# First loads in smaller pieces with x ahead on the scalar engine's queue; the last two slots of the last token tile in halves

## The chip, the cores and the metric

One Trainium2 chip, one core. The time is that of the device for one execution of the whole program, in microseconds (us), the median of three runs. The core has TensorE (PE in the profile, its weight loads PEld), VectorE (DVE), ScalarE (ACT), GpSimd (POOL) and SyncE (SP, which here only issues transfers).

## What is computed

The reference runs two blocks on x, 256 tokens by 2048 columns in float32. The first has a state-space layer (S5) and a sparse-attention layer, the second an attention layer with two kinds of heads and an MLP. Only the two ends matter here:

```python
def s5_mixer(x, w_in, lam_re, lam_im, log_dt, b_re, b_im, c_re, c_im, d_skip, w_glu, b_glu, w_out):
    u, z = jnp.split(x @ w_in, 2, axis=-1)       # the kernel's first work: u, in four groups of columns
    dt = jnp.exp(log_dt.astype(f32))[:, None]     # tables of the state space, from small parameters
    mag = jnp.exp(lr * dt)
    ar = mag * jnp.cos(li * dt)
    ai = mag * jnp.sin(li * dt)
...
def second_block(x, ...):
...
        h = rmsnorm(x, ln2[l])
        x = x + jnp.square(jax.nn.relu(h @ w_mlp_in[l])) @ w_mlp_out[l]
    return rmsnorm(x, ln_f)                        # the kernel's last work
```

## The kernel before

**Weights.** All large matrix products go through one stream of weights. A unit is a block of 2048 by 512 weights in eight slots; a slot holds two row tiles of 128 by 512. SP brings slot after slot into `RAW` (`slot`, line 414). ACT rounds a slot into `WH` (`high`, the group L1195), DVE forms the remainder `WL` (`low`, L1824), and PE multiplies in three passes (high by high, high by low, low by high). One slot's work on PE is called a tick, and `lo_ready` tells PE that the slot's two parts are there. Ticks are numbered through the program; `beside(tau)` on PE and on ACT puts other small work behind tick tau. Each engine runs its own list in the order in which it is written; nothing else sets the order.

**The start.** `WHOLE = 6`: ticks 0 to 5 don't wait for the split. They multiply the raw float32 weights in `whole_tick` (L657), eight instructions a tick. They need x with columns in partitions. PE turns 128 by 128 pieces of x (`transposes`, L639: four for each index i, which is one pair of row tiles, and so one tick), ACT copies each turned pair to `XF` (`x_cols`, L1234, two copies for each i), and the semaphore `tr_tmp` lets the tick of that number start. Before the first transposes PE runs `WARM = 5` matmuls on zeros (L664). x comes in four pieces of 512 columns (`x_piece`, 512 KB), each for two ticks. SP issues the first behind a small piece of the constants, then the weight slots, with x pieces 1 to 3 between them. ACT's queue issues the small parameters (log_dt, lam_re, lam_im).

Beside this run the tables of the state space. PE turns the parameters (`params_turn`, L674), the first of them between the two halves of tick 0; ACT copies them (L1226) and takes an exponential (L1356); then DVE starts a long list of its own (`angles`, L1887, then `turns`, `base_products`, `base_turns`, `factors`, `coefficients`, `powers`, `b_powers`), in which also stand the remainders of x (`rounding_left`, L1865: each waits for ACT's rounding of x, L1241) and those of the weights of ticks 6 to 9 (L1824). ACT's rounding of the first two pairs (`rounded(0, 2)`) stands in its list behind `x_cols(2, 4)`, so behind the copies of x piece 1.

**The end.** In the last unit the work is done for token tile 0 and then for tile 1 in slots 4 to 7 (`tiles_apart`, L581; matmuls of 512 columns, weights moving). For each tile DVE adds the last product to x (L2853), sums squares (L2854), POOL takes the root (`rsqrt`, L2895), and then DVE scales columns 1024 to 1535 (L2857) and scales and multiplies by the gain columns 1536 to 2047 (L2859), while ACT scales columns 0 to 1023 (L1804). The columns 0 to 1535 have been multiplied by the gain before. SP stores the two pieces of DVE (256 KB each), ACT's queue the half of ACT (512 KB). The program ends when SP has seen all six stores land.

## Time and profile before

| | us |
|---|---|
| median of three runs (2005.87 to 2006.30) | 2006.16 |
| span of the profiled execution, first to last instruction | 2003.7 |
| PE busy | 1991.7 |
| DVE busy | 1317.6 |
| ACT busy | 981.9 |
| POOL busy | 73.8 |
| TensorE clock granted, mean | 0.999 |

The span is counted from the first instruction to the last; the median of the runs lies 2.5 us above it, for what stands around the instructions. In a timeline row the first two numbers are the start and the length of a group in us from the span's start, `x8` is how many records it holds (a float32 matmul leaves two records, a transpose one), and brackets tell how long the engine was idle before it and what ended that. A "q" behind an engine's name (SPq, ACTq) marks work of its sequencer, such as issuing a transfer.

### The profile page before, as it was taken

How to read it: one execution, taken by the hardware profiler on the slowest of the kernel's cores; microseconds unless marked ns; L12 is line 12 of the kernel's file. 1: busy time of each engine (PE TensorE's matmuls, PEld its weight loads, DVE VectorE, ACT ScalarE, POOL GpSimd, SP SyncE). 2: the span in 40 equal slices, each digit the busy share in tenths (PEclk: the TensorE clock that was granted, in tenths of full speed). 3: DMA queues.
4: the chain of work that ended last, by engine and by line, in shares of the span. 5: the costliest groups of instructions: out<-in, count | busy, mean ns of one | idle time of the engine just before them, and what ended most of it. 6: DMA issues, size and time to landing. Idle time of an engine off the chain costs nothing.

```text
span 2003.7 us, 30858 instructions
## 1 busy us (share of the span) xinstructions
PE 1991.7 (99%) x11849; PEld 1735.5 (87%) x11849; DVE 1317.6 (66%) x1931; ACT 981.9 (49%) x1444; POOL 73.8 (4%) x84
## 2 busy tenths in 40 slices
PE   9999999999999999999999999999999999999998
PEld 8998789988888888888999988888888888888887
DVE  7998877566666666578767766555555555555555
ACT  5664555354545454455456446544344434434443
POOL 2000132000000000100000001000000000000000
PEclk9999999999999999999999999999999999999999
DMA  9346578546464545756555555566666666666663
GB/s 293 96 152 234 164 214 250 165 131 189 126 195 131 182 145 169 247 154 199 169 168 148 155 171 191 178 189 190 194 188 190 193 191 189 189 195 181 196 192 107
DMA packets 203220, 360.74 MB, mean 180 GB/s; under 512 B 25393, under 2 KB 33937, under 8 KB 202449
## 3 DMA queue, kind: packets, MB, share of 16 engines
q1 hardware_dynamic: 200944, 351.82, 57.5%
q0 software_dynamic: 1664, 5.97, 0.9%
q8 instruction: 94, 1.54, 0.3%
q10 hardware_dynamic: 480, 1.10, 0.1%
q14 instruction: 38, 0.30, 0.0%
...
## 4 chain that ended last, share of the span: by engine, by line
PE 90%; DVE 7%; issue 1%; ACT 1%; DMA 0%; POOL 0%; POOLq 0%; DVEq 0%; ACTq 0%; SPq 0%
PE acc L529 36%; PE acc L533 10%; PE banks L563 9%; PE acc L563 9%; PE banks L529 8%; PE banks L566 4%; PE acc L566 4%; DVE w_high_low L1824 2%; PE banks L983 1%; PE acc L657 1%; PE banks L956 1%; PE acc L581 1%; PE acc L603 1%; PE banks L969 1%; PE banks L1035 1%
## 5 line engine op out<-in xcount | busy, mean ns | idle before, releaser
L1824 DVE TENSOR_TENSOR w_high_low<-raw,w_high_low 128x1024 fp32r<-128x1024 f32 x650 | 794.6, 1231 | 599.6 <-ACT w_high_low L1195 597.2
L1195 ACT ACTIVATE w_high_low<-raw 128x1024 fp32r<-128x1024 f32 x650 | 684.0, 1059 | 707.7 <-PE acc L529 292.9
L529 PE MATMUL acc<-w_high_low,x_high_low 128*128 128x512 f32 x1608 | 387.1, 396 | 0.4 <-DVE w_high_low L1824 0.4
L529 PEld LDWEIGHTS acc<-w_high_low,x_high_low 128*128 128x128 f32 x1608 | 299.5, 188 | 63.0 <-issue 0.8
L529 PE MATMUL acc<-w_high_low,h_high 128*128 128x512 f32 x1088 | 292.1, 390 | 0.1
L533 PE MATMUL acc<-x_high_low,w_high_low 128*128 128x256 f32 x2160 | 273.5, 285 | 0.0
L533 PEld LDWEIGHTS acc<-x_high_low,w_high_low 128*128 128x128 f32 x2160 | 263.4, 191 | 1.6
L563 PE MATMUL acc<-x_high_low,w_high_low 128*128 128x512 f32 x768 | 241.9, 396 | 0.4
L563 PE MATMUL banks<-x_high_low,w_high_low 128*128 128x512 f32 x768 | 241.2, 395 | 0.0
L529 PEld LDWEIGHTS acc<-w_high_low,h_high 128*128 128x128 f32 x1088 | 203.0, 188 | 41.8 <-issue 0.5
L566 PEld LDWEIGHTS banks<-x_high_low,w_high_low 128*128 128x128 f32 x768 | 144.3, 188 | 34.1
L566 PEld LDWEIGHTS acc<-x_high_low,w_high_low 128*128 128x128 f32 x768 | 144.3, 188 | 34.0
L529 PE MATMUL acc<-w_high_low,h_low 128*128 128x512 f32 x544 | 167.6, 389 | 0.0
L566 PE MATMUL acc<-x_high_low,w_high_low 128*128 128x256 f32 x768 | 150.9, 278 | 0.0
L566 PE MATMUL banks<-x_high_low,w_high_low 128*128 128x256 f32 x768 | 150.9, 278 | 0.0
L529 PE MATMUL banks<-w_high_low,h_high 128*128 128x512 f32 x480 | 128.3, 389 | 0.0
L529 PEld LDWEIGHTS acc<-w_high_low,h_low 128*128 128x128 f32 x544 | 102.1, 188 | 21.3
L563 PEld LDWEIGHTS acc<-x_high_low,w_high_low 128*128 128x128 f32 x768 | 117.6, 189 | 1.9 <-DVE x_rows L2205 1.0
L563 PEld LDWEIGHTS banks<-x_high_low,w_high_low 128*128 128x128 f32 x768 | 116.9, 189 | 0.0
L529 PEld LDWEIGHTS banks<-w_high_low,h_high 128*128 128x128 f32 x480 | 90.1, 188 | 18.7
L529 PE MATMUL banks<-w_high_low,h_low 128*128 128x512 f32 x240 | 73.9, 389 | 0.0
L529 PEld LDWEIGHTS banks<-w_high_low,h_low 128*128 128x128 f32 x240 | 45.0, 188 | 9.4
...
## 6 DMA issues: line engine op xcount, KB each, us to landing
raw<-in_b_w_in SPq DMA_DIRECT2D x128, 512.0 KB, 3.8
raw<-in_w_mlp_in SPq DMA_DIRECT2D x128, 512.0 KB, 3.7
raw<-in_w_mlp_out SPq DMA_DIRECT2D x128, 512.0 KB, 4.5
raw<-in_w_in SPq DMA_DIRECT2D x96, 512.0 KB, 4.0
raw<-in_kv_w SPq DMA_DIRECT2D x48, 512.0 KB, 4.2
raw<-in_a_w_in SPq DMA_DIRECT2D x32, 512.0 KB, 6.6
raw<-in_b_w_out SPq DMA_DIRECT2D x32, 512.0 KB, 4.7
raw<-in_w_out SPq DMA_DIRECT2D x32, 512.0 KB, 4.7
```

The lines of the kernel that those rows point to most:

```text
L529: ins_ = nc.tensor.matmul(PAIRS[pair][:, t, :], xa[:, kt + j, t * P:(t + 1) * P], wa[:, k, j, :], start=first and n == 0, stop=last and n ...
L533: ins_ = nc.tensor.matmul(ACC[pair][:, m // 2, (m % 2) * TOK:(m % 2 + 1) * TOK], wa[:, k, j, m * P:(m + 1) * P], xa[:, kt + j, :], start=f ...
L563: nc.tensor.matmul(both, WH[:, k, j, m * P:(m + 1) * P], XX[:, 2 * s + j, :, :].rearrange("p c t -> p (c t)"), start=s == 0 and j == 0, st ...
L566: ins_ = nc.tensor.matmul(both[:, 0:TOK], WL[:, k, j, m * P:(m + 1) * P], XH[:, 2 * s + j, :], start=False, stop=s == SLOTS - 1 and j == 1 ...
L581: ins_ = nc.tensor.matmul(PAIRS[pair][:, t, :], xa[:, kt, t * P:(t + 1) * P], wa[:, s % SPLIT, j, :], start=start and s == SPLIT and j == ...
L603: ins_ = nc.tensor.matmul(PAIRS[group % 2][:, t, :], xa[:, 2 * s + j, t * P:(t + 1) * P], wa[:, k, j, :], start=s == 0 and j == 0 and n == ...
L657: ins_ = nc.tensor.matmul(ACC[0][:, m // 2, (m % 2) * TOK:(m % 2 + 1) * TOK], RAW[:, s, j, m * P:(m + 1) * P], XF[kt // 8][:, kt % 8, :], ...
L956: ins_ = nc.tensor.matmul(BK[n % 2][:, lo:lo + w], QT[:, h, t * P:(t + 1) * P], keys[:, g:g + 1, 0:w].rearrange("p o k -> p (o k)"), start ...
L969: ins_ = nc.tensor.transpose(BK[2][:, b * P:(b + 1) * P], PB_[:, n % 2, b * P:(b + 1) * P], ID)
L983: ins_ = nc.tensor.matmul(BK[3][:, t * P:(t + 1) * P], PTB[:, n % 2, b * P:(b + 1) * P], v[:, k, g * HD:(g + 1) * HD], start=b < 2, stop=b ...
L1195: nc.scalar.activation(WH[:, s % SPLIT, :, :], RAW[:, s, :, :], ACT.Copy).then_inc(hi_ready, WHOLE + 1 if first_one else 1)
L1824: V.tensor_tensor(WL[:, k, :, :], RAW[:, p % SLOTS, :, :], WH[:, k, :, :].bitcast(F32), ALU.subtract).then_inc(lo_ready, WHOLE + 1 if isin ...
```

## The change

At the start, x piece 0 is cut in two. Its first 256 columns are issued by ACT's queue, ahead of the parameters; SP issues slot 0 as two transfers with the rest of x piece 0 between them. PE waits for the first half of x (`x_ahead`), turns only pair 0, and runs tick 0, each half of it when its half of the weights is there. Pair 1 is turned behind tick 0 together with the first parameters; x piece 1 and the second parameters, which were turned behind tick 0, are turned behind tick 1. ACT's list has the copies of pair 1 at the head of what it does beside tick 0. One warming matmul is left out.

At the end, slots 6 and 7 of tile 1 are done for columns 0 to 255 of the last group first, and then for columns 256 to 511 into a bank of their own. DVE adds the whole product so far and squares the first half while PE does the second; then it adds and squares the second half. The gain is multiplied while POOL takes the root. The last scaling is split at column 896: ACT does 0 to 895, DVE 896 to 2047 in one instruction, and each is stored by one transfer.

```diff
--- before.py
+++ after.py
@@ -52,7 +52,8 @@
 LAST_ROOT, LAST_TILE = 6, 3
-WARM = 5
+LAST_COLS = 896
+WARM = 4
@@ -436,8 +438,11 @@
-        x_piece(0)
-        for s in range(SLOTS):
+        first_w = rows_cols(A_IN, 0, 0)
+        sp.dma_start(RAW[:, 0, 0, :], first_w[:, 0, :]).then_inc(w_first, 16)
+        sp.dma_start(X[:, :, 2 * P:COLS], x_in[:, :, 2 * P:COLS]).then_inc(x_first[0], 16)
+        sp.dma_start(RAW[:, 0, 1, :], first_w[:, 1, :]).then_inc(raw_in[0], 16)
+        for s in range(1, SLOTS):
             slot(U_AIN, s, rows_cols(A_IN, 2 * P * s, 0))
@@ -505,19 +510,17 @@
-        for t in range(NT):
-            for c in (2, 3):
-                sp.wait_ge(out_ready, 2 * t + c - 1)
-                cols = slice(c * COLS, (c + 1) * COLS)
-                sp.dma_start(out[0, t * P:(t + 1) * P, cols], X[:, t, cols]).then_inc(stored, 16)
-        sp.wait_ge(stored, 16 * 3 * NT)
+        for n, (t, c0, c1) in enumerate(((0, 2 * COLS, 3 * COLS), (0, 3 * COLS, DM), (1, LAST_COLS, DM))):
+            sp.wait_ge(out_ready, n + 1)
+            sp.dma_start(out[0, t * P:(t + 1) * P, c0:c1], X[:, t, c0:c1]).then_inc(stored, 16)
+        sp.wait_ge(stored, 16 * 5)
@@ -569,10 +572,28 @@
+        def last_halves(pair, kt0, free):
+
+            for half in range(2):
+                cols = slice(half * COLS // 2, (half + 1) * COLS // 2)
+                bank = ACC[0][:, 0, 0:COLS // 2] if half else PAIRS[pair][:, 1, cols]
+                if half:
+                    pe.wait_ge(acc_free, free)
+                for s in (SLOTS - 2, SLOTS - 1):
+                    for j in range(2):
+                        kt = kt0 + 2 * (s - SPLIT) + j
+                        for n, (xa, wa) in enumerate(((HH, WH), (HH, WL), (HL, WH))):
+                            ins_ = nc.tensor.matmul(bank, xa[:, kt, P:2 * P], wa[:, s % SPLIT, j, cols],
+                                                    start=half == 1 and s == SLOTS - 2 and j == 0 and n == 0,
+                                                    stop=s == SLOTS - 1 and j == 1 and n == 2, skip_group_check=True)
+                ins_.then_inc(slot_used if half else tile_full, 2 if half else 1)
+
-        def tiles_apart(unit, pair, kt0, start, xh, xl):
+        def tiles_apart(unit, pair, kt0, start, xh, xl, halves=False):
 
             for t in range(NT):
                 for s in range(SPLIT, SLOTS):
+                    if halves and t and s >= SLOTS - 2:
+                        continue
@@ -647,12 +668,13 @@
-            pe.wait_ge(raw_in[s], 16)
+            if s:
+                pe.wait_ge(raw_in[s], 16)
             pe.wait_ge(tr_tmp, TR_X + s + 1)
             for j in range(2):
                 kt = 2 * s + j
-                if kt == 1:
-                    params_turn(0)
+                if s == 0:
+                    pe.wait_ge(*((raw_in[0], 16) if j else (w_first, 16)))
@@ -663,7 +685,8 @@
         pe.wait_ge(const_in, 16)
-        x_turn(0)
+        pe.wait_ge(x_ahead, 16)
+        transposes(TR_X, X, None, 0, 1)
@@ -777,6 +800,10 @@
             if tau == 0:
+                pe.wait_ge(x_first[0], 16)
+                transposes(TR_X, X, None, 1, 2)
+                params_turn(0)
+            if tau == 1:
                 x_turn(1)
                 params_turn(1)
@@ -1214,6 +1243,8 @@
+        x_in = ins["x"][0].rearrange("(t p) d -> p t d", p=P)
+        act.dma_start(X[:, :, 0:2 * P], x_in[:, :, 0:2 * P]).then_inc(x_ahead, 16)
         act.dma_start(LDT[64:96, :], ins["a_log_dt"][0].rearrange("(s w) -> s w", w=2)).then_inc(dt_in, 16)
@@ -1240,7 +1271,7 @@
-        x_cols(0, 2)
+        x_cols(0, 1)
@@ -1351,6 +1382,7 @@
             if tau == 0:
+                x_cols(1, 2)
                 params_copy(1, 1)
@@ -1801,9 +1833,10 @@
-            nc.scalar.activation(X[:, t, 0:DM // 2], X[:, t, 0:DM // 2], ACT.Copy, scale=RSTD[:, t:t + 1]).then_inc(last_scaled, 1)
+            cols = slice(0, LAST_COLS if t else DM // 2)
+            nc.scalar.activation(X[:, t, cols], X[:, t, cols], ACT.Copy, scale=RSTD[:, t:t + 1]).then_inc(last_scaled, 1)
@@ -2844,27 +2877,47 @@
+        def last_tile():
+            xr = X[:, 1, 3 * COLS:]
+            v.wait_ge(tile_full, LAST_TILE + 1)
+            steps.link(V.scalar_tensor_tensor(xr, PAIRS[3][:, 1, :], RSTD[:, 5:6], xr, ALU.mult, ALU.add))
+            for half in range(2):
+                xr = X[:, 1, 3 * COLS + half * COLS // 2:3 * COLS + (half + 1) * COLS // 2]
+                if half:
+                    v.wait_ge(slot_used, SLOTS * (U_MLP + 32))
+                    steps.link(V.scalar_tensor_tensor(xr, ACC[0][:, 0, 0:COLS // 2], RSTD[:, 5:6], xr, ALU.mult, ALU.add))
+                before_, sum_ = (MS[:, NT:NT + 1], MS[:, 1:2]) if half else (MS[:, NT + 1:NT + 2], MS[:, NT:NT + 1])
...
+            v.wait_ge(ms_rows, LAST_ROOT + 1)
+            xr = X[:, 1, 3 * COLS:]
+            steps.link(V.tensor_tensor(xr, xr, GF[:, 3 * COLS:], ALU.mult))
+            v.wait_ge(rstd_rows, LAST_ROOT + 1)
+            xr = X[:, 1, LAST_COLS:]
+            V.tensor_scalar(xr, xr, RSTD[:, 1:2], None, ALU.mult, ALU.bypass).then_inc(out_ready, 1)
```

In DVE's part tile 0 keeps the old steps under the name `first_tile`, and in the call of the last unit `last_halves` follows `tiles_apart(..., halves=True)`.

PE's list at the start, before (L639 transposes of x, L657 the raw ticks, L674 parameters):

```order
3 L639 MATMUL banks<-constants,x_rows 128x128 [waits x_first0,const_in]
4 L639 MATMUL banks<-constants,x_rows 128x128 x7
5 L657 MATMUL acc<-x_cols_90,raw 128x256 [waits tr_tmp,raw_in0]
6 L657 MATMUL acc<-x_cols_90,raw 128x256 x3
7 L674 MATMUL acc<-constants,param_rows 128x128 [waits ssm_in,rows_set]
8 L657 MATMUL acc<-x_cols_90,raw 128x256 x4
9 L639 MATMUL banks<-constants,x_rows 128x128 [waits x_first1]
10 L639 MATMUL banks<-constants,x_rows 128x128 x7
11 L674 MATMUL acc<-constants,param_rows 128x128 [waits params_in]
12 L657 MATMUL acc<-x_cols_90,raw 128x256 [waits tr_tmp,raw_in1]
13 L657 MATMUL acc<-x_cols_90,raw 128x256 x7
14 L657 MATMUL acc<-x_cols_90,raw 128x256 [waits tr_tmp,raw_in2]
```

and after (L660 transposes, L679 the raw ticks, L697 parameters):

```order
3 L660 MATMUL banks<-constants,x_rows 128x128 [waits x_ahead,const_in]
4 L660 MATMUL banks<-constants,x_rows 128x128 x3
5 L679 MATMUL acc<-x_cols_90,raw 128x256 [waits w_first,tr_tmp]
6 L679 MATMUL acc<-x_cols_90,raw 128x256 x3
7 L679 MATMUL acc<-x_cols_90,raw 128x256 [waits raw_in0]
8 L679 MATMUL acc<-x_cols_90,raw 128x256 x3
9 L660 MATMUL banks<-constants,x_rows 128x128 [waits x_first0]
10 L660 MATMUL banks<-constants,x_rows 128x128 x3
11 L697 MATMUL acc<-constants,param_rows 128x128 [waits ssm_in,rows_set]
12 L679 MATMUL acc<-x_cols_90,raw 128x256 [waits tr_tmp,raw_in1]
13 L679 MATMUL acc<-x_cols_90,raw 128x256 x7
14 L660 MATMUL banks<-constants,x_rows 128x128 [waits x_first1]
```

The eight transposes of x piece 0 have become four, four more stand directly ahead of tick 1, those of x piece 1 directly ahead of tick 2, and the first parameters stand behind all of tick 0.

ACT's list at the start, after, from the copies of pair 1 on (L1265 copies of turned x, L1257 copies of turned parameters, L1388 the exponential that DVE waits for, L1272 rounding of x; before, the same rows stood in the same order, as L1234, L1226, L1356 and L1241):

```order
9 L1265 ACTIVATE x_cols_90<-banks 128x256 [waits tr_full]
10 L1265 ACTIVATE x_cols_90<-banks 128x256
11 L1257 ACTIVATE param_cols<-acc 128x128 [waits params_full]
12 L1388 ACTIVATE ssm_params<-param_cols 128x32 [waits params_done]
13 L1265 ACTIVATE x_cols_90<-banks 128x256 [waits tr_full]
14 L1265 ACTIVATE x_cols_90<-banks 128x256
15 L1265 ACTIVATE x_cols_90<-banks 128x256 [waits tr_full]
16 L1265 ACTIVATE x_cols_90<-banks 128x256
17 L1257 ACTIVATE param_cols<-acc 128x128 [waits params_full]
18 L1272 ACTIVATE x_high_low<-x_cols_90 128x2x256 [waits tr_tmp] x2
```

Nothing moved within this list, but the transposes that its copies of pair 1, and of pairs 2 and 3, wait for are now done by PE one tick later.

The last instructions of DVE, after (L2894 to L2912 are token tile 1, in the lines of the new `last_tile`):

```order
1309 L2894 SCALAR_TENSOR_TENSOR x_rows<-banks,rstd,x_rows 128x512
1310 L2901 ISA normed_rows,mean_squares<-x_rows,mean_squares 128x256
1311 L2901 ISA mean_squares 128x1
1312 L2899 SCALAR_TENSOR_TENSOR x_rows<-acc,rstd,x_rows 128x256
1313 L2901 ISA normed_rows,mean_squares<-x_rows,mean_squares 128x256
1314 L2901 ISA mean_squares 128x1
1315 L2909 TENSOR_TENSOR x_rows<-x_rows,last_gain 128x512
1316 L2912 TENSOR_SCALAR x_rows<-x_rows,rstd 128x1152
```

where before there stood for tile 1:

```order
1309 L2853 SCALAR_TENSOR_TENSOR x_rows<-banks,rstd,x_rows 128x512
1310 L2854 ISA normed_rows,mean_squares<-x_rows,mean_squares 128x512
1311 L2854 ISA mean_squares 128x1
1312 L2857 TENSOR_SCALAR x_rows<-x_rows,rstd 128x512
1313 L2859 SCALAR_TENSOR_TENSOR x_rows<-x_rows,rstd,last_gain 128x512
```

The sum and the squares are in halves of 256 columns, and the two scalings of 512 columns have become a gain and one scaling of 1152.

## Rows read from the trace of the kernel before

**Rows 1.** Page, its first lines: span and busy time of the engines.
```profile
span 2003.7 us, 30858 instructions
...
PE 1991.7 (99%) x11849; PEld 1735.5 (87%) x11849; DVE 1317.6 (66%) x1931; ACT 981.9 (49%) x1444; POOL 73.8 (4%) x84
```

**Rows 2.** Waits of PE in the whole span: total, times, longest, in us.
```profile
PE banks L639 <- DMA x_rows<-in_x: 0.6, 1, 0.6
...
PE acc L657 <- ACT x_cols L1234: 0.4, 1, 0.4
```

**Rows 3.** Transfers issued in 0 to 1.3 us: KB, us to landing.
```profile
x_rows<-in_x SPq DMA_DIRECT2D x1, 512.0 KB, 4.3
constants<-in_consts SPq DMA_DIRECT2D x1, 72.0 KB, 2.2
...
param_rows<-in_a_lam_re ACTq DMA_DIRECT2D x1, 16.0 KB, 4.2
```

**Rows 4.** Timeline of the start, PE and ACT around ticks 0 and 1.
```profile
0.75 0.42 ACTq L1217 DMA_DIRECT2D log_dt_rows<-in_a_log_dt  x1
...
1.20 3.87 PE L664 MATMUL banks<-products_a 128*128 128x256 f32 x10 [1.20 <-DVE products_a L1874]
...
1.21 0.42 SPq L437 DMA_DIRECT2D x_rows<-in_x  x1
...
5.70 1.06 PE L639 MATMUL banks<-constants,x_rows 128*128 128x128 f32 x8 [0.63 <-DMA x_rows<-in_x]
...
6.36 1.21 ACT L1234 ACTIVATE x_cols<-banks 128x256 f32<-128x256 f32 x4 [2.38 <-PE banks L639]
...
7.16 1.97 PE L657 MATMUL acc<-x_cols,raw 128*128 128x256 f32 x8 [0.40 <-ACT x_cols L1234]
...
10.80 1.04 PE L639 MATMUL banks<-constants,x_rows 128*128 128x128 f32 x8
...
11.44 1.21 ACT L1234 ACTIVATE x_cols<-banks 128x256 f32<-128x256 f32 x4 [1.63 <-PE banks L639]
...
11.79 7.07 PE L657 MATMUL acc<-x_cols,raw 128*128 128x256 f32 x32
...
12.67 1.18 ACT L1241 ACTIVATE x_high_low<-x_cols 128x512 fp32r<-128x512 f32 x2
```

**Rows 5.** The same timeline, DVE's list and PE up to tick 9.
```profile
9.84 0.19 DVE L1887 TENSOR_TENSOR ssm_params<-param_cols,ssm_params 128x32 f32<-128x32 f32 x1 [6.82 <-ACT ssm_params L1356]
...
14.01 1.29 DVE L1865 TENSOR_TENSOR x_high_low<-x_cols,x_high_low 128x512 fp32r<-128x512 f32 x2
...
38.66 6.02 PE L533 MATMUL acc<-x_high_low,w_high_low 128*128 128x256 f32 x48
...
40.09 2.39 DVE L1824 TENSOR_TENSOR w_high_low<-raw,w_high_low 128x1024 fp32r<-128x1024 f32 x2
```

**Rows 6.** Waits of DVE between 9.8 and 42 us: total, times, longest.
```profile
DVE x_high_low L1865 <- ACT x_high_low L1241: 0.3, 1, 0.3
```

**Rows 7.** Timeline of the end, token tile 1.
```profile
1995.77 0.62 PE L581 MATMUL banks<-w_high_low,h_high 128*128 128x512 f32 x2
1996.23 0.39 PE L581 MATMUL banks<-w_high_low,h_low 128*128 128x512 f32 x1
...
1996.65 0.75 DVE L2853 SCALAR_TENSOR_TENSOR x_rows<-banks,rstd,x_rows 128x512 f32<-128x512 f32 x1 [1.33 <-PE banks L581]
...
1997.44 0.75 DVE L2854 CUSTOM_DVE_ANT_0 normed_rows<-x_rows,mean_squares 128x512 f32<-128x512 f32 x1
...
1998.87 0.49 DVE L2857 TENSOR_SCALAR x_rows<-x_rows,rstd 128x512 f32<-128x512 f32 x1 [0.67 <-POOL rstd L2895]
...
2000.11 0.37 ACTq L1806 DMA_DIRECT2D out<-x_rows  x1
```

**Rows 8.** Groups of DVE by line and shape: count, busy, mean ns, idle before.
```profile
L1843 DVE CUSTOM_DVE_ANT_0 banks<-banks,constants 128x256 f32<-128x256 f32 x48 | 22.3, 465 | 0.0
...
L2760 DVE SCALAR_TENSOR_TENSOR x_high_low<-banks,param_cols,x_high_low 128x256 fp32r<-128x256 f32 x16 | 6.5, 474 | 0.4 <-ACT x_high_low L1748 0.4
```

46 lines of the change are left out of this document (26 added, 20 removed).

## The prediction

> **What bounds the kernel now.** The page's first lines come first: PE is busy 1991.7 of 2003.7 us [rows 1], so whatever moves PE's first or last instruction moves the end one for one, and nothing in between has slack to give back. The list of PE's waits says the same: only tenths of a microsecond anywhere, the largest at the start, for x and then for ACT's copy of the turned x [rows 2]. The change touches only the two ends, so the stretch before PE's first real multiply and the stretch behind its last are to be costed, and one question more: does every engine that PE needs shortly after the start keep up? For that the timeline of the first 45 us is read for DVE [rows 5]. DVE starts its list at 9.84 us, when ACT has the first parameters, and from there to 41.3 us it waits once, for 0.3 us [rows 6]. So in this stretch DVE bounds itself, and the remainder of the weights of tick 9 stands in that list: L1824 runs from 40.09, two in 2.39 us, the first done at 41.3. PE runs ticks 8 and 9 from 38.66, 48 matmuls in 6.02 us, so it asks for tick 9 at 38.66 + 2.95 = 41.6. The margin is 0.3 us. That is the row on which this prediction turns: a PE that is early there gains 0.3 us at most, and a late DVE is paid in full.
>
> **Start, step 1: x arrives earlier.** The first transfer of x (512 KB) is issued at 1.21 and lands 4.3 us later; PE starts turning at 5.70 and multiplies at 7.16 [rows 3, 4]. Now 256 KB go out at 0.75, where the first parameter stood on ACT's queue. Early bound: 72 KB took 2.2 us and 512 KB took 4.3 [rows 3]; by bytes 256 KB take 3.1 and land at 3.9, but PE then still warms up: ten records from 1.20 to 5.07, two of them fewer now, some 4.6. Late bound: half of slot 0 travels beside it, so the same 512 KB are under way and the time stays 4.3, landing at 5.05, PE at 5.2. I take PE at 4.85, nearer the early end, since the second queue starts at once and its half doesn't wait for all of the other. The first multiply then comes at 4.85 + 1.46 = 6.3 in place of 7.16: -0.85 (between -1.05 and -0.5). The warming matmul left out costs nothing: PE waited 0.63 us behind it.
>
> The Trainium skill (Trainium Kernel Development and Optimization, Key Constraints) says that transfers issued from several engines share the same 16 DMA engines, and that this saves only the time of issue. By that rule the late bound would hold, and the result would be 0.35 us higher than the one below. No row of before shows two large loads side by side on two queues.
>
> **Step 2: PE waits for ACT twice.** Turning a pair, copying it on ACT and starting the tick takes 1.46 us where nothing hides it: 5.70 to 7.16, with ACT starting 0.66 after PE [rows 4]. Before, this was paid once; pair 1 was turned in its shadow, and pairs 2 and 3 were turned a whole tick ahead. Between tick 0 and tick 1 there stand 0.99 us (10.80 to 11.79), and ticks 1 and 2 run on as one row. Now pair 1 is turned directly ahead of tick 1 and pair 2 directly ahead of tick 2. Ahead of tick 1: 1.45 in place of 0.99, less 0.1 for the parameters that no longer stand inside tick 0: +0.35. Ahead of tick 2: 1.45 where nothing stood, with the refilled pipeline +1.5. Together +1.85. The transposes of x pieces 2 and 3 stay where they were. With step 1 PE asks for everything behind tick 2 1.0 us later than before, so at tick 9 at 42.6.
>
> **Step 3: DVE starts later.** Its list began 9.84 - 7.16 = 2.7 us behind the first multiply. Now the parameters are turned behind all of tick 0 and copied behind ACT's copies of pair 1: tick 0 3.54, then 0.64 until ACT starts, 0.6 for two copies, 0.3 for the parameters' copy, 0.26 for the exponential: 5.3 behind 6.3, so 11.6. That is +1.8.
>
> **Step 4: and then it waits for ACT.** At 14.01 DVE takes the remainder of x (L1865), which needs ACT's rounding L1241. That started at 12.67, 1.87 us behind the first transpose of x piece 1, and half of its 1.18 is needed [rows 4, 5]. It stands behind the copies of that piece, which PE now turns behind tick 1: 6.3 + 3.54 + 1.45 + 3.5 = 14.8. The rounding starts at 16.7, its first half is done at 17.35, DVE goes on at 17.4. Alone DVE would have been there at 15.8. So the list is late by 17.4 - 14.0 = 3.4 us from here. Its one later wait, 0.3 us, goes, since ACT is then less late than DVE [rows 6]. The remainder for tick 9 is done at 41.3 + 3.4 - 0.3 = 44.4.
>
> **Sum of the start.** PE asks at 42.6 and gets it at 44.4; before it went on at 41.6. Start: +2.8 us. Queued behind tick 9 on PE is all the rest of the program, and PE has no idle time in it that could give this back.
>
> **The end.** PE: 12 matmuls of 512 columns at 0.23 (1995.77 to 1996.23 are two) become 24 of 256 at 0.123 (6.02 for 48): +0.2 [rows 5, 7]. DVE behind the last matmul: sum and squares of 512 columns take 0.75 each; of 256 columns the same kinds took 0.47 [rows 7, 8]: -0.55. The root is there 0.4 us earlier. The first half's work (0.75 + 0.47) lies beside PE's last 12 matmuls (1.5 us), and so costs nothing; were that cover gone, it would cost up to 1.2. Then the stores. The gain (512 columns, no more than the 0.75 of the scaling with gain) lies beside POOL's root but ends some 0.1 behind it. DVE's scaling of 512 columns took 0.49; for 1152 it is between 0.85 (a fixed part of 0.2) and 1.1 (by columns). Before, DVE's first store could go when its first scaling ended, 1999.36; now its only store goes between 1999.45 and 1999.65, while ACT's goes 0.5 earlier than 2000.11 (0.4 of the root, 0.1 of 128 fewer columns). The same 1 MB is stored. If bytes bound it, the end is +0.1 to +0.3; if the last queue to start bounds it, -0.5. I take 0.0 between the two, since one transfer moves each way.
>
> **The rivals.** (1) *x comes late on ACT's queue, and the kernel is slower.* The 16 KB of lam_re, second on that queue, took 4.2 us, as long as 512 KB on SP's [rows 3]. If ACT's queue gets so small a share beside the weights, x lands later, and every microsecond is paid: all of steps 2 to 4 hang on the first multiply. From a landing at 5.9 us on the result is slower by over 0.2%; with 6.6 it is 2.8 + 1.9 = +4.7, 2010.9. For it speaks that row; against it that lam_re was behind another transfer and x now is first. (2) *DVE doesn't hold PE at tick 9*, because the rounding isn't late or PE is later than I think. It decides when DVE's lateness is under 1.3 us. What is left is PE's own +1.0: 2007.2. Against it speaks the margin of 0.3 us and a DVE without waits. (3) *The gain shows*: ACT's copies are hidden after all, step 2 costs nothing and DVE keeps its margin: -0.85 at the start and -0.5 at the end, 2004.8. Against it speaks that the 1.46 us stand in the trace for just this sequence.
>
> **How the numbers follow.** The profiled span of 2003.7 becomes 2006.5. The runs lie 2.5 us above the span for what surrounds it, which the change doesn't touch: 2006.16 + 2.8 + 0.0 = 2009.0. Its own range takes in the bounds of step 1 (-0.2 to +0.35), the end (-0.5 to +0.3) and some 0.3 for steps 2 to 4: 2008.0 to 2010.0. About 0.2%, 4.0 us, is what a measurement of this kernel can tell from no change; so this forecast is within it, though on the slow side. Chances: forecast 0.62, rival 1 0.13, rival 2 0.12, rival 3 0.08, something else 0.05. Slower by over 0.2%, above 2010.2: rival 1, the rest and a tail of the forecast's, 0.16. Faster by over 0.2%, under 2002.1: no case reaches it, 0.02. The range leaves out rival 3 and the far part of rival 1: 2007.0 to 2010.5.
>
> **What would show it.** Step 1: the first transpose between 4.6 and 5.2 us. Step 2: PE waits of some 0.9 us ahead of tick 1 and 0.5 ahead of tick 2, on ACT's copies. Steps 3 and 4: DVE's list starts at about 11.6, and L1865's successor waits 1.5 us for the rounding. The sum: PE waits at tick 9 for DVE, for 1 us or more together with shorter waits at ticks 6 and 7, and goes on near 44.4. The end: a root 1.8 us behind the last matmul in place of 2.2, and both stores issued within 0.3 us. If DVE goes on at L1865 without a wait, step 4 is wrong and the sum falls by about 1.5; if the granted clock is low in the first ticks, all of it is too low.

## The result, and the profile after

The changed kernel takes 2012.76 us (2010.95 to 2012.93, six runs) where the kernel before takes 2006.23: 1.0031 times as long, with a 95% interval of 1.0021 to 1.0041. The forecast was 2009.0, with a range up to 2010.5: so it had the direction right, but its +2.8 us is less than half of the 6.5 us measured. The six runs fall into two groups, two near 2011 and four near 2012.8. The profiled execution is one of the first group, 2010.95 us with a span of 2009.1, and all readings below are of it unless another is named. Nine later runs of the same code (below) gave 2010.9 to 2011.8 eight times and 2012.9 once. So the median of 2012.76 is one of the upper group, and what follows explains first the 5.4 us of the lower one.

The page's first lines and PE's list of waits, as in [rows 1, 2] (total, times, longest, in us):

```profile
span 2009.1 us, 30884 instructions
...
PE 1992.7 (99%) x11859; PEld 1735.7 (86%) x11859; DVE 1325.1 (66%) x1934; ACT 981.6 (49%) x1444; POOL 73.8 (4%) x84
```

```profile
PE acc L536 <- DVE w_high_low L1857: 2.5, 2, 1.8
PE acc L679 <- DMA raw<-in_a_w_in: 1.4, 2, 0.9
...
PE acc L679 <- ACT x_cols L1265: 1.0, 2, 0.7
```

Two waits are new, for DVE's remainders of the weights (L1857 is before's L1824) and for the first weights, and the wait for ACT's copies of x has grown from 0.4 to 1.0 us. The timeline of PE at the start answers [rows 4, 5] (start, us busy, and in brackets the idle time before; the last row of the first block is cut by the window's end, tick 1 goes on behind it):

```profile
4.43 0.60 PE L660 MATMUL banks<-constants,x_rows 128*128 128x128 f32 x4
5.97 1.97 PE L679 MATMUL acc<-x_cols,raw 128*128 128x256 f32 x8 [0.95 <-DMA raw<-in_a_w_in]
8.39 1.99 PE L679 MATMUL acc<-x_cols,raw 128*128 128x256 f32 x8 [0.45 <-DMA raw<-in_a_w_in]
10.22 0.60 PE L660 MATMUL banks<-constants,x_rows 128*128 128x128 f32 x4
10.66 0.27 PE L697 MATMUL acc<-constants,param_rows 128*128 128x128 f32 x1
11.66 2.61 PE L679 MATMUL acc<-x_cols,raw 128*128 128x256 f32 x11 [0.73 <-ACT x_cols L1265]
```

```profile
34.27 6.27 PE L536 MATMUL acc<-x_high_low,w_high_low 128*128 128x256 f32 x48 [1.84 <-DVE w_high_low L1857]
...
46.30 3.13 PE L536 MATMUL acc<-x_high_low,w_high_low 128*128 128x256 f32 x24 [0.68 <-DVE w_high_low L1857]
```

PE turns x 1.3 us earlier than before and multiplies 1.2 us earlier, and yet it goes on at tick 9 at 46.3 in place of 41.6, 4.7 us late. By tick 4 PE itself is 1.5 us late (25.36, before 23.90); the rest comes in its two waits for DVE, ahead of ticks 6 and 9, and since DVE hands over tick 9's weights only at 46.2, it is DVE's lateness that counts. DVE's own timeline of the same stretch, the four rows that matter, and POOL's one row:

```profile
11.98 0.19 DVE L1920 TENSOR_TENSOR ssm_params<-param_cols,ssm_params 128x32 f32<-128x32 f32 x1 [3.34 <-ACT ssm_params L1388]
...
17.75 1.29 DVE L1898 TENSOR_TENSOR x_high_low<-x_cols,x_high_low 128x512 fp32r<-128x512 f32 x2 [1.50 <-ACT x_high_low L1272]
...
25.42 0.43 DVE L1912 TENSOR_SCALAR rotation_base<-rotation_base 128x512 f32<-128x512 f32 x1
25.89 1.99 DVE L1943 TENSOR_SCALAR rotation_base<-rotation_base 128x512 f32<-128x512 f32 x1
```

```profile
25.58 4.04 POOL L2944 MEMSET c_powers<- 128x2048 f32 x2 [17.02 <-PE banks L660]
```

The list starts 2.1 us late, waits 1.5 us for ACT's rounding (late by 3.7), and then one operation of 0.43 us takes 1.99 (late by 5.3), while POOL zeroes c_powers. In the kernel before, the same operation and the same zeroing stood apart:

```profile
22.14 0.43 DVE L1910 TENSOR_SCALAR rotation_base<-rotation_base 128x512 f32<-128x512 f32 x1
```

```profile
24.12 3.55 POOL L2891 MEMSET c_powers<- 128x2048 f32 x2 [15.56 <-PE banks L639]
```

The end, which answers [rows 7]:

```profile
2001.40 0.28 PE L586 MATMUL acc<-w_high_low,h_low 128*128 128x256 f32 x1
...
2002.83 0.69 DVE L2909 TENSOR_TENSOR x_rows<-x_rows,last_gain 128x512 f32<-128x512 f32 x1
2002.88 1.06 POOL L2948 TENSOR_TENSOR rstd<-mean_squares,minus_half 128x1 f32<-128x1 f32 x1 [3.83 <-DVE mean_squares L2901]
2004.03 1.04 ACT L1837 ACTIVATE x_rows<-x_rows,rstd 128x896 f32<-128x896 f32 x1 [3.74 <-POOL rstd L2948]
2004.05 0.82 DVE L2912 TENSOR_SCALAR x_rows<-x_rows,rstd 128x1152 f32<-128x1152 f32 x1 [0.52 <-POOL rstd L2948]
...
2005.11 0.37 ACTq L1839 DMA_DIRECT2D out<-x_rows  x1
```

POOL's root starts earlier behind the last matmul (1.2 us behind its end, before 1.7) but takes 1.06 in place of 0.56, so that it ends 2.26 behind it (before 2.2). So the budget of the profiled execution is: tick 9 +4.7, from there to the last matmul +0.4 (some 0.2 of it are the halves), from the last matmul to the end of the span +0.3 (7.4 in place of 7.1). Together +5.4, the difference of the spans.

### The profile page after: what moved, and what is told of

The parts are those of the page before. It is cut to its first block, busy times and chain, and to the rows that moved or that the text cites. A ratio compares the mean times of both kernels' runs of the same rounds, so it can differ in the third digit from the quotient of the medians.

```text
span 2009.1 us, 30884 instructions
## 1 busy us (share of the span) xinstructions
PE 1992.7 (99%) x11859; PEld 1735.7 (86%) x11859; DVE 1325.1 (66%) x1934; ACT 981.6 (49%) x1444; POOL 73.8 (4%) x84
## 3 DMA queue, kind: packets, MB, share of 16 engines
q0 software_dynamic: 1664, 5.97, 0.9%
## 4 chain that ended last, share of the span: by engine, by line
PE 88%; DVE 9%; issue 2%; ACT 1%; DMA 0%; SPq 0%; POOL 0%; POOLq 0%; DVEq 0%; ACTq 0%
PE acc L532 35%; PE acc L536 9%; PE banks L566 9%; PE acc L566 9%; PE banks L532 8%; PE banks L569 4%; PE acc L569 4%; DVE w_high_low L1857 2%; PE banks L1010 1%; PE banks L983 1%; PE acc L602 1%; PE acc L624 1%; PE banks L996 1%; PE banks L1062 1%; PE banks L1086 0%
## 5 line engine op out<-in xcount | busy, mean ns | idle before, releaser
L1857 DVE TENSOR_TENSOR w_high_low<-raw,w_high_low 128x1024 fp32r<-128x1024 f32 x650 | 797.0, 1235 | 598.3 <-ACT w_high_low L1224 595.9
```

Of the source, the lines that this page charges most:

```text
L1857: V.tensor_tensor(WL[:, k, :, :], RAW[:, p % SLOTS, :, :], WH[:, k, :, :].bitcast(F32), ALU.subtract).then_inc(lo_ready, WHOLE + 1 if isin ...
```

## The experiments

All times below are medians, and each is set beside runs of the kernel before on the same chip at the same time (2005.7 to 2006.0). Not all experiments ran on the same chip, so two of them are compared by their distance from the kernel before. The intervals of the ratios are about 0.001 to either side, 2 us; differences of a few tenths are read from medians and from traces, and are called so.

### The start alone, and what in it costs

**e1_start.** The diff without its end part.

> The start part of the change alone (split loads, x ahead on ACT's queue, one warming matmul fewer, pair 1 and the parameters turned behind tick 0); the end is as in the kernel before. Theory A: in the profiled run of the changed kernel PE reaches tick 9 4.7 us late (46.30 in place of 41.64), and that is all the start costs. So this kernel takes 2006.2 + 4.7 = 2010.9 us in the same kind of run, and its PE starts tick 9 at about 46.3. The changed kernel's runs fall in two groups, near 2011 and near 2012.8; if the second group is one more DVE operation that waits for a zeroing of POOL (1.9 us each), this kernel shows it as well, and its other group lies at 2012.8 less 0.5. Rival B: the lateness of the first ticks is given back later in the program, and the end part makes most of the loss: then this kernel is within 1.5 us of 2006.2.

Measured: 2011.08 us (2009.83 to 2012.3, 7 runs) against 2005.86, ratio 1.0028 (1.0017 to 1.0040); PE at tick 9 at 45.79 in the profiled run of 2009.83. The start costs 5.2 us in the median and nothing of it is given back: the span minus the start of tick 9 is 1962.2 here, and before 2003.7 - 41.6 = 1962.1. Theory A holds. Two of the seven runs, 2012.2 and 2012.3, form an upper group here as well, and e2_end (below) has none above 2007.1, so that group comes from the start, not from the end.

**e3_memset_later.** As e1_start, and POOL's zeroing waits for DVE:

```
         pool.wait_ge(tr_full, TR_X + 8)
+        pool.wait_ge(tab_dve, 3)
         for i in range(2):
             GP.memset(CX[i][:, :, :, :, :, :], 0.0).then_inc(zeroed, 1)
```

> As e1_start, but POOL's two zeroings of c_powers wait until DVE is through with its rotation_base operations. Theory A (DVE's TENSOR_SCALAR of 128x512 stands still for as long as POOL zeroes: 1.99 us at 25.89 in the changed kernel, 0.43 in the kernel before): that operation takes 0.43 again, the remainder for tick 9 is done 1.56 us earlier, at 44.7, PE starts tick 9 at 44.7, and the time is 2006.2 + 3.1 = 2009.3 us in all runs, with no second group. Rival B (the 1.99 us come from something else, such as a late operand): the time stays that of e1_start, 2010.9 or 2012.5.

Measured: 2009.13 us (2008.47 to 2010.52, 10 runs), 2.0 under e1_start in the median and 1.4 from fastest run to fastest. Its DVE and POOL rows:

```profile
27.14 0.43 DVE L1893 TENSOR_SCALAR rotation_base<-rotation_base 128x512 f32<-128x512 f32 x1
27.61 0.43 DVE L1924 TENSOR_SCALAR rotation_base<-rotation_base 128x512 f32<-128x512 f32 x1
27.95 1.29 DVE L1879 TENSOR_TENSOR x_high_low<-x_cols,x_high_low 128x512 fp32r<-128x512 f32 x2
```

```profile
28.16 3.55 POOL L2906 MEMSET c_powers<- 128x2048 f32 x2 [19.57 <-DVE rotation_base L1924]
```

The operation is back at 0.43, and so is POOL's zeroing at 3.55 (4.04 beside it). TENSOR_TENSOR at 27.95 runs beside the zeroing and is not longer than elsewhere. Theory A holds in its main point. That there would be no second group was wrong: two of ten runs, the profiled one among them, lie at 2010.5, and this profile tells why (below, under the clock).

**e8_memset_collides.** The other direction: the kernel before, with POOL's early zeroings moved beside DVE's rotation_base operations.

```
+        pool.wait_ge(tr_full, TR_X + 6)
         GP.memset(BB[:, :, :, :, :, :], 0.0).then_inc(zeroed, 1)
```

> The kernel before, but POOL zeroes b_powers, tap_blocks and decay only behind the turning of the sixth pair of x, at about 19.7 us instead of 6.0, beside DVE's rotation_base operations. Theory A (a TENSOR_SCALAR of DVE stands still while POOL zeroes): one of the TENSOR_SCALAR between 19.3 and 20.2 takes some 1.3 to 1.8 us in place of 0.43, while TENSOR_TENSOR beside the same zeroing keeps its 0.69; the list is late by about 1.3 us, tick 9 by about 1.0, time 2006.9 to 2007.4 us. Rival B (no such standing still): 2005.9, and all TENSOR_SCALAR at 0.43.

Measured: 2006.82 us (2005.84 to 2008.01, 10 runs) against 2005.99, ratio 1.0004 (0.9995 to 1.0013). The profiled run is a low one, 2005.9. There the zeroing started at 20.01, inside the second of two operations (19.82 to 20.25), which kept its length; the two that started beside a zeroing got longer:

```profile
19.36 0.89 DVE L1879 TENSOR_SCALAR rotation_base<-rotation_base 128x512 f32<-128x512 f32 x2
...
21.74 0.53 DVE L1879 TENSOR_SCALAR rotation_base<-rotation_base 128x512 f32<-128x512 f32 x1
22.30 0.92 DVE L1910 TENSOR_SCALAR rotation_base<-rotation_base 128x512 f32<-128x512 f32 x1
```

```profile
20.01 1.98 POOL L2887 MEMSET b_powers<- 128x2048 f32 x1 [13.94 <-PE banks L639]
21.94 1.01 POOL L2888 MEMSET tap_blocks<- 128x768 f32 x1
22.89 0.39 POOL L2889 MEMSET decay<- 128x8 f32 x1
```

Both of the later ones are longer than 0.43, and each of POOL's zeroings is longer too: 8 elements took 0.39 here, 0.14 in the kernel before. In the changed kernel it is the same: the operation at 25.42 was running when the zeroing began at 25.58 and kept its 0.43, the next one took 1.99. TENSOR_TENSOR at 20.28 and 21.01 stood beside the same zeroing at 0.69 each. In eight of ten runs the time is about 0.6 us or more over the kernel before's median; that in them the zeroing started ahead of the earlier operation is likely, but they have no trace. Theory A's mechanism holds in the trace. Its sizes don't: no operation took 1.3 us, and the 0.8 us of the medians are less than its 0.9 to 1.4 and within the interval.

The Trainium skill (SBUF — State Buffer, Who interferes with whom) states this rule: VectorE and GpSimd share a pair of SBUF ports as an exclusive lock, and `tensor_scalar` and `copy` can run in a mode that takes it, while a VectorE instruction with two SBUF inputs contends only with a GpSimd instruction that reads SBUF. These rows agree with both halves of it: TENSOR_SCALAR at 1.99 beside a zeroing, TENSOR_TENSOR at 0.69. It is a rule by which such a meeting has a price, and the forecast didn't weigh it.

**e5_rounding_first.** As e1_start, and ACT rounds pairs 0 and 1 ahead of its copies of pairs 2 and 3:

```
+                rounded(0, 2)
                 x_cols(2, 4)
                 params_copy(2, 0)
-                rounded(0, 2)
```

> As e1_start, but ACT rounds pairs 0 and 1 of x before it copies pairs 2 and 3, so DVE's first remainders of x find their operand. Theory A: DVE's wait of 1.50 us at 16.2 goes; the list is then only 2.1 us late and its last rotation_base operation ends before POOL's zeroing starts at 25.6, so that the stall of 1.56 goes too. DVE is then 4.93 - 1.50 - 1.56 = 1.9 us late at tick 9, PE itself asks 1.5 us late: tick 9 at 43.2, time 2006.2 + 1.6 = 2007.8 us. Rival B (the wait is only replaced by another, since the copies of pairs 2 and 3 now come later and PE's tick 2 with them): no gain against e1_start, 2010.9 or more. Rival C (only the wait goes, the stall stays): 2009.4.

Measured: 2007.34 us (2007.15 to 2008.91, 10 runs), 3.7 under e1_start in the median and 2.7 from fastest run to fastest, ratio to the kernel before 1.0008 (0.9998 to 1.0017). DVE waits for no rounding of x, and its operation takes 0.43 at 26.02. POOL's zeroing, which starts when PE has turned the last pair, then comes behind it (27.32). The profiled run is the highest of the ten, 2008.91; in it everything from tick 1 on stands some 2 us later (below, under the clock). Theory A holds: the wait of 1.5 us was worth twice its length or more, since it moved the list by just so much that it met the zeroing.

**e4_order.** As e1_start with all its loads; pair 1 and the parameters are turned between the halves of tick 0, pairs 2 and 3 directly behind it:

```
                 if s == 0:
+                    if j:
+                        pe.wait_ge(x_first[0], 16)
+                        transposes(TR_X, X, None, 1, 2)
+                        params_turn(0)
                     pe.wait_ge(*((raw_in[0], 16) if j else (w_first, 16)))
...
             if tau == 0:
-                pe.wait_ge(x_first[0], 16)
-                transposes(TR_X, X, None, 1, 2)
-                params_turn(0)
-            if tau == 1:
                 x_turn(1)
                 params_turn(1)
```

> As e1_start with its loads, but PE turns pair 1 and the first parameters between the two halves of tick 0, and pairs 2 and 3 directly behind tick 0 as in the kernel before. Theory A (the loss is one of order on PE, not of the loads): the first multiply stays at 5.97, the first parameters are turned at about 8.1 and DVE's list starts at about 9.4 in place of 11.98 (before: 9.84), without the waits for rounding and without the stall; tick 9 at 41.3, time 2005.9 us (between 2005.5 and 2006.3). Rival B (the loads in small pieces land later, slot 1 at 9.56 in place of 8.29, and PE pays for that): tick 1 starts later than 11.79 and the time is 2007 us or more.

Measured: 2006.14 us (2005.45 to 2007.59, 10 runs), 4.9 under e1_start, ratio 1.0003 (0.9993 to 1.0013). Seven runs lie at 2005.5 to 2006.4, three at 2007.5. In the profiled run, a low one, the list starts at 9.64, tick 1 at 11.71 and tick 9 at 41.56. So theory A: the loads in smaller pieces and on ACT's queue cost nothing that can be measured, apart from what lifts the three high runs; the loss comes from where PE does the turning. The parameters were turned at 8.70, not at 8.1, and not because they had landed late:

```profile
5.09 3.56 DVE L1890 COPY param_rows<-log_dt_rows 32x128 f32<-32x128 f32 x1 [3.95 <-DMA log_dt_rows<-in_a_log_dt]
```

This copy of 32x128 took 0.22 us in the kernel before. Now log_dt lands at 5.1 us instead of 2.8, and the copy runs until 8.64, when POOL's zeroings of b_powers, tap_blocks and decay (6.01 to 8.57) are over. The changed kernel's copy does the same (5.10 to 8.64), and there POOL's rows are:

```profile
4.91 0.57 POOL L2937 DMA_DIRECT2D head_gains<-in_diff_head_norm  x1
5.48 0.54 POOL L2937 DMA_DIRECT2D head_gains<-in_sb_head_norm  x1
6.01 1.82 POOL L2939 MEMSET b_powers<- 128x2048 f32 x1
```

So it is the same standing still, with one thing open: the copy starts 0.9 us ahead of the first zeroing, while POOL issues its last two transfers, and doesn't end there. In the kernel before it took 0.22 at 2.80, also while POOL was issuing transfers. Why it didn't end before 6.01 is not shown. In the changed kernel it costs nothing, because the parameters are turned only at 10.66.

### The second group: the clock in tick 0

In the profiled runs of e3_memset_later (2010.52 us, where eight others lay at 2008.5 to 2009.4) and of e5_rounding_first (2008.91, others 2007.2 to 2007.9), tick 0 took longer. The timeline of PE in e3_memset_later:

```profile
1.20 3.78 PE L670 MATMUL banks<-products_a 128*128 128x256 f32 x8 [1.20 <-DVE products_a L1888]
4.77 1.06 PE L644 MATMUL banks<-constants,x_rows 128*128 128x128 f32 x4
6.58 5.52 PE L663 MATMUL acc<-x_cols,raw 128*128 128x256 f32 x16 [0.75 <-ACT x_cols L1247]
```

16 matmuls in 5.52 us, where e1_start and the kernel before need 3.7 and 3.8; seven of the first eight have 634 ns records, as the warming matmuls at 1.2 GHz do, the last ones 379 as at 2.4 GHz. The trace's record of the granted clock starts, at its full level, only at 10.26 us here (10.29 in e5_rounding_first), but at 4.1 to 6.3 us in every profile of the changed kernel that there is, and at 4.15 in the kernel before. PE had gone idle for 0.75 us at 5.83 without the clock having risen. That alone doesn't make a late rise: in h4_changed_look (below) PE went idle for the same 0.75 us at 5.84, and the record starts at 6.34. The changed kernel has one warming matmul fewer, and the forecast said that this costs nothing.

**g1_warm5.** The changed kernel with `WARM = 5`.

> The changed kernel with one thing undone: five warming matmuls, as before, in place of four. Theory W: the granted clock rises to its full level only after PE has been kept busy for a while; in the kernel before it rose at 4.15 us, in the profiled run of the changed one at 4.07, but in two of four profiled variants with four warming matmuls PE had gone idle first and the clock rose only at 10.3 us, with tick 0 taking 5.4 us in place of 3.6. That is the second group of the changed kernel's runs. With five warming matmuls at least 8 of 10 runs lie near 2011 us and the median falls from 2012.8 to about 2011.0; spans near 2009.1. Rival X (the groups come from when x and the weights land, or from how DVE and POOL meet): the groups and the median of about 2012 stay.

Measured: 2011.58 us (2011.03 to 2011.98, 8 runs): no run near 2012.8, as theory W had it, but none under 2011.0 either, and the median is 0.6 above the 2011.0 expected. In the profiled run the warming lasts until 5.83 and the first multiply stands at 7.31.

**g2_warm4.** The kernel before with `WARM = 4`.

> The kernel before with one warming matmul fewer, nothing else. Theory W: a part of its runs, some 3 to 7 of 10, finds the clock low when tick 0 starts; tick 0 then takes 5.4 us in place of 3.6, and since the margin at tick 9 is 0.3 us these runs take some 1.5 us more, 2007.4; the others stay at 2005.9. Rival Y (my forecast: the matmul left out costs nothing, since PE waited 0.63 us behind it): all runs at 2005.9, like the kernel before.

Measured: 2005.92 us (2005.42 to 2007.48, 10 runs) against 2005.99. The median stays, as my forecast had it, but three runs lie at 2006.96 to 2007.48, and none of the 31 runs of the kernel before beside them is above 2006.86 (of the 28 beside the first four experiments one was, at 2007.32). One matmul less costs nothing in seven runs of ten and about 1 to 1.5 us in three. The profiled run is a low one although its clock record starts only at 7.13: turning x takes 1.90 us there in place of 1.06, and the first multiply stands at 7.32 in place of 7.16.

**i2_before_warm3.** The kernel before with `WARM = 3`.

> The kernel before with three warming matmuls in place of five. Theory W: more of the runs than with four (3 of 10 above 2006.9) find the low clock; the low tick 0 costs up to 1.9 us less the margin of 0.3 at tick 9: median 2006.5 to 2007.5. My forecast's view (a warming matmul costs nothing as long as PE waits behind it): 2005.8, like the kernel before.

Measured: 2007.36 us (2005.99 to 2008.1, 10 runs) against 2005.72, ratio 1.0007 (0.9997 to 1.0017). In its profiled run PE is idle 1.9 us ahead of x:

```profile
6.03 1.94 PE L639 MATMUL banks<-constants,x_rows 128*128 128x128 f32 x8 [1.91 <-DMA x_rows<-in_x]
7.96 2.74 PE L657 MATMUL acc<-x_cols,raw 128*128 128x256 f32 x8
```

Turning takes 1.94 us in place of 1.06 and half of tick 0 takes 2.74 in place of 1.97. The clock's record starts at 9.54, and tick 9 at 43.2 in place of 41.6. Theory W holds here: in the kernel before, leaving out two warming matmuls costs 1.6 us in the median although PE waits behind them, and nine of the ten runs lie above all 17 runs of the kernel before beside them. Three of the ten spend 0.3 to 1.1 us more than the usual 1.8 outside the span, the profiled one the most; by spans the loss is 1.3 us.

**h2_filled.** The changed kernel, its four warming matmuls kept and two more where PE was idle:

```
         transposes(TR_X, X, None, 0, 1)
+        for n in range(2):
+            nc.tensor.matmul(BK[3][:, 0:TOK], T1[:, 0, 0:P], T1[:, 0, 0:TOK], start=True, stop=True)
```

> The changed kernel, four warming matmuls as it has, and two more between the turning of pair 0 and the first multiply, where PE was idle for 0.95 us. Theory W: the low clock of tick 0 needs this idle time; without it no run lies near 2012.8, all are between 2010.7 and 2011.8, median 2011.2. Rival X: 2 or more of the runs lie above 2012.3, as in the changed kernel (5 of 13 so far).

Measured: 2011.15 us (2010.65 to 2011.49, 8 runs), no run above 2011.5, as theory W had it.

**i1_warm3.** The changed kernel with `WARM = 3`.

> The changed kernel with three warming matmuls in place of four. Theory W: PE is idle sooner and longer before its first multiply, so most runs find the low clock there: the median is 2012.8 or a little more, and the profiled run shows matmuls of 634 ns in tick 0, the clock rising near 10 us, DVE's list starting at about 13.7 in place of 11.98, the operation of 1.99 us as before, tick 9 near 48.2. Rival X (the second group is not the clock's): the median stays at 2011.3 with the same share of high runs.

Measured: 2011.53 us (2010.31 to 2012.2, 8 runs), clock's record from 5.45, tick 0 at 379 ns. Here theory W missed: one warming matmul less did not make the low clock the rule.

**a1_changed_again, h3_changed_look, h4_changed_look.** The changed kernel itself once more, 7, 1 and 1 runs.

> The changed kernel once more, for a second look at its two groups of runs. Theory W: each run near 2012.8 is one in which the granted clock had not risen by the time PE went idle ahead of its first multiply. If the profiled run falls there, its records show matmuls of 634 ns in tick 0 in place of 379, a rise of the clock near 10.3 us, DVE's list starting at about 13.7 in place of 11.98, still with the 1.99 us operation, and PE at tick 9 near 48.2 in place of 46.3. Rival X: a run near 2012.8 has a tick 0 of 3.6 us and loses its 1.9 us elsewhere, for instance in a second DVE operation that stands still.

> The changed kernel, one more profile, in case it falls into the group near 2012.8. Theory W: if the time is near 2012.8 the clock rises near 10.3 us, tick 0 takes 5.4 us and DVE's list starts at about 13.7; if it is near 2011 the clock rises before 7 us.

> As h3_changed_look, one more profile with the same expectation: near 2012.8 with a late rise of the clock, or near 2011 with an early one.

Measured: 2011.33 (2010.9 to 2012.91), 2011.18 and 2011.31 us. No profiled run fell into the upper group. Their clock records start at 4.74, 5.00 and 6.34 us; PE turns x at 4.76 to 4.78 in them and multiplies at 6.11 to 6.58.

So: that a late rise of the clock costs 1 to 2 us and makes high runs is shown by one profiled run each of e3, e5 and i2. That it is what lifted four of the first six runs of the changed kernel is only argued: the amount fits (5.5 in place of 3.7 us for tick 0), and g1 and h2 are without high runs, but with one high run among the nine later ones of the changed kernel the absence in eight proves little, and i1 speaks against it. Which chip the first six ran on is not on record, and the nine later ones ran on two, so that the share of high runs could depend on that too. This stays open.

The last profiles show one more cost. Of h3_changed_look, by stretches (us, PE busy, granted clock, DMA share, GB/s):

```profile
34.00:36.00 2.00, 1.65 (x13) 0.93 1.06 424
36.00:38.00 2.00, 2.00 (x11) 0.50 0.83 321
38.00:40.00 2.00, 2.00 (x15) 0.72 0.12 28
```

Behind PE's 1.84 us of waiting for DVE at tick 6 the granted clock falls to half, 1.2 GHz, and tick 7 runs at that. a1, h2 and i1 show the same; the first profile, e1, g1 and h4 don't. From the start of tick 6 to that of tick 9 it takes 12.4 us (34.35 to 46.74) in place of 12.0 (34.27 to 46.30): a wait may cost more than its length, here 0.4 us more.

### The end

**e2_end.** The end part alone, the start as before.

> The end part of the change alone (last two slots of the last token tile in halves, squares by halves, gain beside the root, 896 columns on ACT and 1152 on DVE); the start is as before. From the profile of the changed kernel: PE's last matmul 0.25 later, the root done 2.26 us behind it in place of 2.22 although it starts earlier (POOL's power took 1.06 in place of 0.56 beside DVE's gain), last store issued at the same distance, its landing 0.4 later. Theory E: +0.5 us, 2006.4 against 2005.9. My forecast was 0.0 (between -0.5 and +0.3).

Measured: 2006.64 us (2006.27 to 2007.06, 11 runs) against 2005.99, +0.65, ratio 1.0003 (0.9994 to 1.0012), so theory E's +0.5 and not the 0.0 of the forecast, as far as medians tell; the root takes 1.06 again and ends 2.26 behind the last matmul's end.

**e6_halves_only.** e2_end without the new scaling: sum and squares in halves, then DVE's two operations, ACT's 1024 columns and the three stores as before (of the diff, DVE's part).

```
...
-            v.wait_ge(ms_rows, LAST_ROOT + 1)
-            xr = X[:, 1, 3 * COLS:]
-            steps.link(V.tensor_tensor(xr, xr, GF[:, 3 * COLS:], ALU.mult))
             v.wait_ge(rstd_rows, LAST_ROOT + 1)
-            xr = X[:, 1, LAST_COLS:]
-            V.tensor_scalar(xr, xr, RSTD[:, 1:2], None, ALU.mult, ALU.bypass).then_inc(out_ready, 1)
+            xr = X[:, 1, 3 * COLS:]
+            V.tensor_scalar(X[:, 1, 2 * COLS:3 * COLS], X[:, 1, 2 * COLS:3 * COLS], RSTD[:, 1:2], None,
+                            ALU.mult, ALU.bypass).then_inc(out_ready, 1)
+            V.scalar_tensor_tensor(xr, xr, RSTD[:, 1:2], GF[:, 3 * COLS:], ALU.mult, ALU.mult).then_inc(out_ready, 1)
```

> The end in halves, but scaling, gain and stores as before: DVE has no work beside POOL's last root, three stores for the last token tile. Theory E (POOL's power takes 1.06 us instead of 0.56 because DVE multiplies by the gain at the same time): the power takes 0.56 again and is done 1.75 us behind the last matmul (2.22 before, 2.26 in e2_end); with PE's +0.25 the end is 0.2 us earlier than before, 2005.8 against 2006.0, and 0.8 below e2_end. Rival F (the power is longer for another reason, such as where its operands lie): it stays at 1.06, and the time at 2006.3 or more.

Measured: 2005.52 us (2005.19 to 2005.97, 11 runs) against 2005.78, 0.26 under it in the median (ratio 0.9999, 0.9990 to 1.0008), and 0.9 further down than e2_end. POOL's root:

```profile
1998.24 0.56 POOL L2936 TENSOR_TENSOR rstd<-mean_squares,minus_half 128x1 f32<-128x1 f32 x1 [3.82 <-DVE mean_squares L2890]
```

With no DVE work beside it the root takes 0.56 and ends 1.76 behind the last matmul's end (1997.04), just what the forecast had. So the halves seem to pay, by less than the interval, and the gain put beside the root takes back their 0.5 us: there DVE's TENSOR_TENSOR has two inputs in SBUF and POOL's instruction reads SBUF, the second case of the rule that the Trainium skill states (SBUF — State Buffer, Who interferes with whom). Theory E holds for the root. The other 0.4 us lie behind it, in the scalings and stores, which e6 put back in the same step; no run has them apart.

### Two versions with a better start

**f1_x_first_on_sp.** The kernel before, with x's first 256 columns ahead of slot 0 on SP's own queue, pair 1 turned inside tick 0 and one more warming matmul behind the turning of pair 0. SP's part of the diff:

```
-        x_piece(0)
+        sp.dma_start(X[:, :, 0:2 * P], x_in[:, :, 0:2 * P]).then_inc(x_ahead, 16)
         for s in range(SLOTS):
             slot(U_AIN, s, rows_cols(A_IN, 2 * P * s, 0))
+            if s == 0:
+                sp.dma_start(X[:, :, 2 * P:COLS], x_in[:, :, 2 * P:COLS]).then_inc(x_first[0], 16)
```

> The kernel before, with only this: SP loads the first 256 columns of x ahead of slot 0 and the next 256 behind it, slot 0 stays in one piece, ACT's queue as before; PE turns pair 0, runs one more warming matmul, starts tick 0 and turns pair 1 and the first parameters between its halves. My theory of the start (PE and DVE are both 0.3 us from binding at tick 9, so both must come earlier for a gain): first multiply at 6.3 in place of 7.16, first parameters turned at 8.4 in place of 8.97, DVE's list at 9.3, tick 9 at 41.1 in place of 41.6, time 0.5 us under the kernel before: 2005.5 against 2006.0. Rival G (smaller pieces land later in sum, as slot 1 at 9.56 in place of 8.29 in the changed kernel): first multiply after 6.8 or tick 1 after 11.8, no gain, or slower by up to 0.5.

Measured: 2006.27 us (2005.79 to 2006.66, 11 runs) against 2005.78: rival G. x is there at 4.83, but slot 0's weights only at 7.14, the clock's record starts at 5.71 and so the warming lasts until 5.8; the first multiply stands at 7.18. Tick 0 then carries pair 1's turning as well, and tick 1 starts at 12.27 (11.79 before), tick 9 at 42.1.

**f2_both_ends.** f1 with the end of e6.

> f1_x_first_on_sp with the end of e6_halves_only. If both theories hold the gains add: 0.5 + 0.2 = 0.7 us under the kernel before, 2005.3 against 2006.0; if only one holds, 0.2 or 0.5.

Measured: 2005.79 us (2005.31 to 2006.17, 11 runs) against 2005.78: 0.5 under f1, where the end alone gave 0.26 in e6, and no gain of the start.

**h1_order_filled.** The changed kernel's loads, the order of e4, two warming matmuls in the idle stretch as in h2, the end of e6.

> The changed kernel's loads with the order of e4_order on PE, two more warming matmuls between the turning of pair 0 and the first multiply, and the end of e6_halves_only. Theory W (3 of 10 runs of e4_order lay 1.5 us above the rest, because PE went idle before the clock had risen): with PE kept busy no run lies more than 0.7 us above the fastest. e4_order's other runs were 0.3 us under the kernel before, the halves gave 0.26: median 0.5 us under the kernel before, 2005.3 against 2005.8, and the first version that is faster than both. Rival X: the high runs stay (2007), median as before or above.

Measured: 2005.39 us (2005.07 to 2006.35, 11 runs) against 2005.68, ratio 0.9999 (0.9990 to 1.0008). The runs at 2007.5 that e4 had are gone, but three of the eleven lie more than the expected 0.7 above the fastest, the highest 1.3. It is 0.3 under the kernel before in the median, which is less than such a measurement can establish, and some 6 us under the changed kernel, which is well established.

## Why the prediction was wrong, point by point

**What bounds the kernel: right.** Span minus tick 9 is the same to 0.2 us (1962.1 to 1962.2) in before and in e1, e3, e4, e5 and f1, which keep its end; the margin of 0.3 us at tick 9 was the row on which it turned.

**Step 1, x earlier: about right; the second half of the weights was left out.** PE turned at 4.43 and multiplied at 5.97 (forecast 4.85 and 6.3), a gain of 1.2 us that lies beyond the bound of 1.05; in the three later profiles the multiply stands at 6.11 to 6.58. With half of slot 0 beside it x took 3.5 us, not the 4.3 of the late bound. In the first profile the wait ahead of the multiply ended with the weights, at 5.84; in the later ones it ended with ACT's copy, 1.35 to 1.8 us behind the first turning, so the weights cost little there. But tick 0 waited 0.45 us more for the second half of slot 0 and took 4.25 us in place of 3.54. So PE's own lateness was 1.5 us by tick 4, not 1.0. DVE hid this.

**Step 2, two waits on ACT: right.** 0.73 and 0.29 us, tick 2 at 16.6 (forecast 16.2 to 16.3).

**Step 3, DVE's list: right.** 11.98, forecast 11.6.

**Step 4, the rounding: right.** DVE waited the forecast 1.5 us and went on at 17.75, forecast 17.4; e5 shows that it hung on the order of ACT's list.

**The sum of the start: the failing step.** The prediction said "the remainder for tick 9 is done at 41.3 + 3.4 - 0.3 = 44.4", which takes for granted that a list that DVE bounds itself moves as a whole. It doesn't: the operation at 25.89 takes 1.56 us longer when it meets POOL's zeroing, whose own start hangs on PE's turning and not on DVE. With 0.35 from steps 3 and 4 and these 1.56 the sum is 46.3, as measured (46.24). The margin between DVE's last TENSOR_SCALAR and the zeroing was 24.12 - 22.57 = 1.55 us before; a list that is late by 3.7 while PE's turning of the last pair is late by 1.5 closes it. That the two would meet could have been read from two rows; what a meeting costs stands in no row of before.

**The end: the second failing step.** PE's +0.2 and DVE's -0.5 came as forecast. The gain beside POOL's root was taken as free and cost 0.5; and two stores of 448 and 576 KB issued within 0.3 us landed later than before's three (3.6 us from the last issue to its landing, 3.2 before). 0.65 to 0.7 in place of 0.0.

**The warming matmul at no cost: wrong as a statement.** One left out costs nothing in most runs and about 1 to 1.5 us in some (g2), two cost 1.6 us in the median (i2). The prediction named the sign itself ("if the granted clock is low in the first ticks, all of it is too low") and gave it no term. How much of the 1.8 us between the profiled run and the median of 2012.76 it explains is open.

**The base.** Time minus span is 1.8 us (1.75 to 1.95) in every run of these comparisons but three of i2, not 2.5. By that the profiled execution of before was one of some 2005.5 us, under all six of its first runs, so the forecast's 2009.0 already held 0.7 us of the spread between runs. Like with like, the forecast was +2.8 on the span and the profile showed +5.4: 1.6 for the zeroing, 0.35 for steps 3 and 4, 0.7 for the end.

**The rivals.** Rival 1's condition (a landing of x from 5.9 on) did not come: x landed at 4.3. Its number, 2010.9, is that of the profiled run by chance. Rival 2 fell with the sum. Rival 3 didn't come.
